# Up projection: 512- and 256-column matmuls by turns in place of eight and eight

## What is computed

```python
h2 = rmsnorm(x, norm2_g[l])
x = x + jnp.square(jax.nn.relu(h2 @ w_up[l])) @ w_down[l]    # w_up: 2048 x 8192, w_down: 8192 x 2048
```

## Time and profile before

| | us |
|---|---|
| median of 3 runs | 2070.12 (2068.88 to 2070.39) |
| the profiled execution | 2069.04 |
| its span, first to last instruction | 2067.1 |
| TensorE matmuls busy | 2061.8 |
| TensorE weight loads busy | 1733.5 |
| VectorE busy | 1267.3 |
| ScalarE busy | 990.7 |

### The profile page before, as it was taken

One profiled execution on the slowest core, in us unless ns is written; L12 is line 12 of the kernel. 1 busy time (PEld: TensorE's weight loads), 2 busy tenths in 40 slices (PEclk: granted clock), 3 DMA queues, 4 the chain that ended last, 5 costly groups with the idle time before them and its releaser, 6 DMA issues.

```text
span 2067.1 us, 26774 instructions
## 1 busy us (share of the span) xinstructions
PE 2061.8 (100%) x10762; PEld 1733.5 (84%) x10762; DVE 1267.3 (61%) x1646; ACT 990.7 (48%) x1328; POOL 191.7 (9%) x196
## 2 busy tenths in 40 slices
PE   9999999999999999999999999999999999999999
PEld 7887788888888888888888877888888888888887
DVE  7767566655565556556677775665655655665664
ACT  6557644443443444344455586444434434434442
POOL 6253100000000000001023531000000000000000
PEclk9999999999999999999999999999999999999999
DMA  9477866666666666666665689666666666666663
GB/s 301 136 229 194 225 184 184 191 191 192 189 192 194 187 190 193 193 185 193 183 178 148 205 203 242 176 183 190 192 192 190 192 194 187 191 193 192 186 193 122
DMA packets 207451, 396.64 MB, mean 192 GB/s; under 512 B 13674, under 2 KB 22352, under 8 KB 207328
## 3 DMA queue, kind: packets, MB, share of 16 engines
q1 hardware_dynamic: 202640, 379.52, 61.9%
q0 software_dynamic: 4512, 15.33, 4.0%
q10 hardware_dynamic: 176, 0.09, 0.0%
HBM read 377.95 MB, written 2.12 MB: 184 GB/s over the span
## 4 chain that ended last, share of the span: by engine, by line
PE 99%; DMA 0%; SPq 0%; DVE 0%; issue 0%
PE psum L496 40%; PE psum L516 23%; PE psum L500 20%; PE psum L519 12%; PE psum L531 1%; PE psum L603 1%; PE psum L582 0%; PE psum L628 0%; PE psum L590 0%; PE psum L588 0%; DMA x<-in_x_dram 0%; PE psum L638 0%; PE psum L619 0%; PE psum L620 0%; PE psum L618 0%; PE psum L640 0%
## 5 line engine op out<-in xcount | busy, mean ns | idle before, releaser
L894 DVE TENSOR_TENSOR w_lo<-raw_ring,w_hi 128x1024 fp32r<-128x1024 f32 (+1 forms) x692 | 850.9, 1231 | 680.8 <-ACT w_hi L715 679.4
L715 ACT CAST w_hi<-raw_ring 128x1024 fp32r<-128x1024 f32 (+1 forms) x720 | 749.7, 1042 | 995.3 <-PE psum L500 604.1
L516 PE MATMUL psum<-xt,w_hi 128*128 128x512 f32 x2048 | 512.9, 392 | 0.0
L496 PE MATMUL psum<-w_hi,ht_hi 128*128 128x512 f32 x1280 | 501.8, 392 | 0.0
L496 PE MATMUL psum<-w_hi,ht_lo 128*128 128x512 f32 x1280 | 498.6, 390 | 0.0
L516 PEld LDWEIGHTS psum<-xt,w_hi 128*128 128x128 f32 x2048 | 368.8, 189 | 66.3
L500 PE MATMUL psum<-w_lo,ht_hi 128*128 128x512 f32 x1280 | 342.5, 389 | 0.0
L519 PEld LDWEIGHTS psum<-xt,w_lo 128*128 128x128 f32 x2048 | 279.4, 190 | 19.9
L519 PE MATMUL psum<-xt,w_lo 128*128 128x256 f32 x2048 | 285.6, 282 | 0.0
L500 PEld LDWEIGHTS psum<-w_lo,ht_hi 128*128 128x128 f32 x1280 | 240.3, 188 | 50.3
L496 PEld LDWEIGHTS psum<-w_hi,ht_hi 128*128 128x128 f32 x1280 | 240.4, 188 | 49.6 <-issue 1.0
(11 more groups left out here) (144 smaller groups left out, 968.2 us busy)
## 6 DMA issues: line engine op xcount, KB each, us to landing
raw_ring<-in_w_up_dram SPq DMA_DIRECT2D x256, 512.0 KB, 3.7
raw_ring<-in_w_down_dram SPq DMA_DIRECT2D x256, 512.0 KB, 3.7
raw_ring<-in_w_in_dram SPq DMA_DIRECT2D x128, 512.0 KB, 4.7
raw_ring<-in_w_out_dram SPq DMA_DIRECT2D x64, 512.0 KB, 4.8
w_lo<-raw_ring POOLq DMA_DIRECT2D x28, 512.0 KB, 5.8
raw_ring<-in_w_in_dram SPq DMA_DIRECT2D x16, 256.0 KB, 2.8
x<-in_x_dram SPq DMA_DIRECT2D x8, 256.0 KB, 7.5
out_dram<-x SPq DMA_DIRECT2D x3, 512.0 KB, 2.7
```

The source lines that it names most:

```text
L496: pe.matmul(bank[r][:, 0:cols], t[:, kt, r * P:(r + 1) * P], w_hi[:, slot, j, 0:cols], start=first and j == 0 and n == 0, stop=False, skip ...
L516: pe.matmul(bank[:, f, :], w_hi[:, w, j, f * P:(f + 1) * P], both, start=kt == 0, stop=False, skip_group_check=True)
L715: act.copy(w_hi[:, u % AHEAD, :, 0:cols], raw_ring[:, u % RAWS, :, 0:cols]).then_inc(hi_ready, 1)
L894: dve.tensor_tensor(w_lo[:, u % AHEAD, :, 0:cols], raw_ring[:, u % RAWS, :, 0:cols], w_hi[:, u % AHEAD, :, 0:cols].bitcast(F32), ALU.subtr ...
```

## The change

In `up_unit` the two loops over the eight (k-tile, block) pairs become one. The wait for the unit's lo part moves ahead of it, and in the loop each 512-column matmul is followed by the 256-column one of the same block, into the same bank.

```diff
@@ -510,12 +510,11 @@
                     pe.wait_ge(evicted[p], pl.evictions(chunk))
                 pe.wait_ge(hi_ready, pl.unit(u + 1))
                 tiles = [(2 * k + j, f, slot, j) for j in range(2) for f in range(4)]
+                unit_is_split(pl, u)
                 for kt, f, w, j in tiles:
                     both = xt_both[:, kt, :, :].rearrange("p h q -> p (h q)")
 
                     pe.matmul(bank[:, f, :], w_hi[:, w, j, f * P:(f + 1) * P], both, start=kt == 0, stop=False, skip_group_check=True)
-                unit_is_split(pl, u)
-                for kt, f, w, j in tiles:
                     mm = pe.matmul(bank[:, f, 0:SEQ], w_lo[:, w, j, f * P:(f + 1) * P], xt[0][:, kt, :], start=False,
                                    stop=kt == KT - 1, skip_group_check=True)
                 mm.then_inc(unit_done, 1)
```

## The result

The change made the kernel slower by 0.4%: 2077.69 us in the median of 6 runs (2077.03 to 2078.94) against 2070.05 in 6 runs of the kernel before, ratio 1.0039 with a 95% interval of 1.0028 to 1.0049. The forecast was 2065.2 us. The time lies inside the range of 2053 to 2079, but on the other side of no change: only rival B had that sign.

A forecast was written before the change was run, and what follows sets the result against it. The tensor engine was taken to bound the kernel, through distances between matmul starts. The new order gave -4.9 us and all other terms nothing, so 2065.2 us against the median of 2070.12, range 2053 to 2079.

The forecast's parts named there:

- rival B: Up projection: each wide matmul pays its worst step, 235 ns, the narrow 120; 355 ns a pair, 2082 us; chance 0.20.
- Step 2: Up projection: wide and narrow matmuls adding into the same psum bank twice in a row, cost 0.
- Step 3: Wait for the lo split, moved 1.8 us earlier ahead of the unit's first matmul: 5.3 us of cover, cost 0.
- Step 4: Separate L511 semaphore instruction, one per unit, 256, hidden behind queued matmuls: cost 0, upper bound 10.7 us.
- Step 5: The rest, weight and ring slots, queues, transfers and DMA load: nothing.
- step 1: Up projection's order, sixteen width changes a unit: wide excess and narrow gain cancel at 346.7 ns a pair, -4.9 us.
- Rival A: Up projection: nothing changes, disturbed steps of 232 and 117 ns last, 349 ns a pair, 2070 us; chance 0.23.
- Rival C: Up projection: larger gain as weight loads no longer pile up, 340 to 344 ns a pair, about 2055 us; chance 0.17.

The follow-up runs named there:

- causes, stretch 1: By turns as in the change, but in this stretch the narrow matmul adds into the next block's bank: 90.44 us, as in the change.
- the kernel with the way in: The change, with W N W W N N (W wide, N narrow) heading each stretch and behind the second transposes: 2063.93 us, ratio 0.9972 to the kernel before.
- entries by stretch: The change, with the first unit of six stretches beginning in another order: four took 90.42 to 90.44 us, two 88.75 and 88.76.
- orders: Wait ahead as in the change, another order of wide and narrow matmuls in each stretch: 89.07 us (every second unit turned) to 90.40 (by turns).
- widths: By turns as in the change, with other column widths in six stretches: 231.2 (256 and 128) to 437.7 ns a pair (512 and 448).

## Why the prediction was wrong

**Right.** What bounds (the distances between matmul starts), the reading of 226.7 and 120 ns, of the 20 ns for two changes of width, and of the first steps behind one (233 and 113 to 114 ns in the trace of before). Step 2: adding into one bank twice in a row is free (causes, stretch 1). Step 3: no up unit waits for its lo part, and the wait by itself measured 0.9999. The cover was thinner than the 5.3 us of the forecast, though, because TensorE's queue takes the wait ahead of the matmuls: in the changed kernel the first one (L480) stands at 325.6 us and its unit's first matmul at 329.49, while the lo part is ready at 324.16 (322.93 + 1.23), 1.4 us ahead of the wait. Step 4's price of nothing; only the line was named wrongly, it is L480 that has 256 semaphore instructions, not L511. For the same reason the L511 instruction at 746.6 belongs not to the unit at 746.85, the last of its chunk, but to the chunk start at 749.65, and the 46 are more than the 32 chunk starts: 22 of them stand in the two stretches with transposes. Step 5: nothing else moved but 0.6 us at the start.

**Wrong: step 1**, "each matmul as the first after a change", so that the wide step's excess and the narrow one's gain cancel at 346.7 ns a pair. I had read the first step behind a long run of the other width and applied it to matmuls whose history is a mixture. The steps went 232 and 118, 241 and 120, 235 and 114. In these three pairs the wide steps are 28 ns over the undisturbed ones and the narrow ones only 8 ns under: they don't cancel. The mean pair is 353.3 ns, +4.2 on the 349.1 of before where -2.5 was forecast, 8.4 us in all. In the trace of before no wide step of the up units is over 236 ns, but for those right behind transposes, so 241 could not be read there.

The forecast's value turned up elsewhere. 346.7 is the pair of the short cycle, where excess (11 ns in two pairs) and gain (11 ns) do cancel; its -4.9 us is what the up units of the kernel with the way in gave, and its 2065.2 is 1.3 us from that kernel's median. That is luck: the forecast had no cycle in it, and its steps are not those of the short one (233 and 117, 231 and 112). What I did not see is that two cycles exist, and that the plain change runs in the long one everywhere but for the two units behind the first transposes of each layer.

**Rival B** (355 ns a pair, 2082 us) had the sign, and +11.9 us where the up units measured +8.4; its 2082 us lay outside the range all the same. Its reason was only half right: the disturbance never settles, but neither is the wide step always the worst one nor the narrow one held at 120. **Rival A** (349 ns, the mean of the disturbed steps) fell: the cycles have means of their own. In the changed kernel 512 columns took 226 to 241 ns in the up units (more only right behind transposes), by what went before. **Rival C** (340 to 344 ns) fell: no order settled under 2773 ns a unit, the sum of the undisturbed streams.

## What to carry to other kernels

Where TensorE has no waits, the time is the distances between matmul starts, and with a weight load for every matmul these depended here on the widths of several matmuls before; price a new order by running it, not by adding up first steps. Keep matmuls of one width together in long runs: turning every second group round halves the changes, and it gained 0.15% here without relying on a cycle. If widths must alternate, read the repeating steps in the trace and try other first orders: the same loop ran at 353 or at 347 ns a pair for hundreds of matmuls depending on one swap of neighbours at its head.

## What was not expected of the hardware

A stream of alternating 512- and 256-column matmuls has two stable cycles, of three pairs (1060 ns) and of two (693 ns). A single W W N N in the middle of a stretch changed the short one into the long one, and it stayed; W N W W N N changed either into the other. Undisturbed steps were the columns over 2.4 GHz plus 13.3 ns at 512, 384 and 256 columns; a 128-column matmul between 512-column ones took 60 ns and the wide one 280. What inside the engine carries the history over some five matmuls stays open: the runs rule out the bank, the tensors, the semaphores and the clock, and leave the widths, but not which part of the path from weight load to psum they act on. Every run had a weight load for every matmul, so whether the cycles need it is not tested. They were the same on other chips of this kind: the short cycle took 88.75 us for a stretch on two chips (entries by stretch; turns with the way in), and the first stretch of a layer by turns, transposes included, 91.21 us on two (orders, widths).
